# A two-part transformer on one core: recurrent block reordered, attention matmuls issued for two heads at a time

## The reference

```
for l in range(DEPTH):                                   # first block, DEPTH = 2
    h = rmsnorm(x, g_pre_mix[l])
    ...splits of h @ w_in[l]: attention (8 heads of 64), pooling, gating unit, convolution, gate logits
    merged = sum of 4 branches, each times sigmoid(gate)
    x = x + rmsnorm(merged @ w_out[l], g_post_mix[l])
    h = rmsnorm(x, g_pre_ffn[l])
    f = (silu(h @ w_ffn_gate[l]) * (h @ w_ffn_up[l])) @ w_ffn_down[l]
    x = x + rmsnorm(f, g_post_ffn[l])

# second block: recurrent block, MLP, attention of 16 heads of 64 over shared keys and values, MLP
u = rmsnorm(x) @ w_in; gate, rec = halves of u
rec = causal convolution of 4 taps + bias
r, i = sigmoid(rec @ w_gate + b)                         # 8 blocks of 128 channels
a = exp(-8 r softplus(-lam)); b = sqrt(1 - a*a) * (i * rec)
h = scan over time of h = a*h + b;  out = (gelu(gate) * h) @ w_out
```

## Time and profile before

| | us |
|---|---|
| median of 3 runs | 2925.27 (2917.92 to 2926.51) |
| the profiled execution's own time | 2922.88 |
| its span | 2921.2 |
| TensorE busy | 2798.7, mean granted clock 0.978 |
| GpSimd busy | 1336.7 |
| VectorE busy | 1254.6 |
| ScalarE busy | 1057.2 |

### The profile page before, as it was taken

One profiled execution on the slowest core, in us unless ns is written; L12 is line 12 of the kernel. 1 busy time (PEld: TensorE's weight loads), 2 busy tenths in 40 slices (PEclk: granted clock), 3 DMA queues, 4 the chain that ended last, 5 costly groups with the idle time before them and its releaser, 6 DMA issues.

```text
span 2921.2 us, 34310 instructions
## 1 busy us (share of the span) xinstructions
PE 2798.7 (96%) x12222; PEld 2233.8 (76%) x12222; DVE 1254.6 (43%) x1679; ACT 1057.2 (36%) x1555; POOL 1336.7 (46%) x1032
## 2 busy tenths in 40 slices
PE   8899998999998999997999988799999999999999
PEld 6677776888876777775888866588888885688887
DVE  5555455212246554555221267753224227552222
ACT  4344433222243344433222345433224346532222
POOL 5345542444443444453444444444444436544443
PEclk9999999999999999998999999899999997999999
DMA  4233222233332333321333322233333220133333
GB/s 136 79 94 99 89 88 71 87 95 100 94 95 80 94 94 94 94 88 60 98 95 100 96 84 80 65 94 96 98 93 129 80 83 4 37 94 95 100 93 101
DMA packets 72697, 259.13 MB, mean 89 GB/s; under 512 B 8192, under 2 KB 9088, under 8 KB 72448
## 3 DMA queue, kind: packets, MB, share of 16 engines
q1 hardware_dynamic: 71280, 254.17, 28.7%
q10 hardware_dynamic: 1296, 3.28, 0.3%
HBM read 255.31 MB, written 2.10 MB: 88 GB/s over the span
## 4 chain that ended last, share of the span: by engine, by line
issue 40%; PE 32%; POOL 24%; DVE 2%; ACT 1%; POOLq 0%; DVEq 0%
POOL w_lo L316 12%; POOL w_lo L318 12%; PE ps L764 9%; PE ps L766 9%; PE ps L765 9%; PE ps L864 2%; PE ps L852 1%; DVE XS L1648 1%; DVE fb L1647 1%; PE ps L845 1%; PE ps L1140 1%; PE ps L1142 0%; PE ps L1141 0%; ACT w_hi L345 0%; PE ps L1086 0%
## 5 line engine op out<-in xcount | busy, mean ns | idle before, releaser
L316 POOL TENSOR_TENSOR w_lo<-w_raw,w_hi 128x512 fp32r<-128x512 f32 x476 | 636.0, 1336 | 1526.0 <-ACT w_hi L345 1525.2
L764 PE MATMUL ps<-H_hi,w_hi 128*128 128x512 f32 x2240 | 905.0, 404 | 35.7 <-POOL w_lo L318 21.2
L765 PE MATMUL ps<-H_lo,w_hi 128*128 128x512 f32 x2240 | 877.0, 392 | 0.0
L766 PE MATMUL ps<-H_hi,w_lo 128*128 128x512 f32 x2240 | 876.6, 391 | 0.0
L345 ACT ACTIVATE w_hi<-w_raw 128x1024 fp32r<-128x1024 f32 x476 | 499.9, 1054 | 536.6 <-DMA w_raw<-w_all 536.2
L318 POOL TENSOR_TENSOR w_lo<-w_raw,w_hi 128x512 fp32r<-128x512 f32 x476 | 650.8, 1367 | 0.0
L764 PEld LDWEIGHTS ps<-H_hi,w_hi 128*128 128x128 f32 x2240 | 423.5, 189 | 150.6 <-POOL w_lo L318 25.7
L765 PEld LDWEIGHTS ps<-H_lo,w_hi 128*128 128x128 f32 x2240 | 423.9, 189 | 97.0 <-issue 12.2
L766 PEld LDWEIGHTS ps<-H_hi,w_lo 128*128 128x128 f32 x2240 | 423.3, 189 | 89.8
L764 PE MATMUL ps<-Y_hi,w_hi 128*128 128x512 f32 x1168 | 458.7, 393 | 31.6 <-POOL w_lo L318 27.2
L766 PE MATMUL ps<-Y_hi,w_lo 128*128 128x512 f32 x1168 | 456.1, 390 | 0.0
(11 more groups left out here) (232 smaller groups left out, 2588.9 us busy)
## 6 DMA issues: line engine op xcount, KB each, us to landing
w_raw<-w_all SPq DMA_DIRECT2D x476, 512.0 KB, 3.6
X<-xT SPq DMA_DIRECT2D x8, 256.0 KB, 6.7
rel_bias<-bias ACTq DMA_DIRECT2D x1, 2048.0 KB, 9.0
outT<-X SPq DMA_DIRECT2D x8, 256.0 KB, 3.2
sguw<-sgu_wT ACTq DMA_DIRECT2D x2, 256.0 KB, 4.6
sgub<-sgu_b ACTq DMA_DIRECT2D x2, 128.0 KB, 4.8
sgug<-sgu_g ACTq DMA_DIRECT2D x2, 128.0 KB, 5.5
CS<-cossin SPq DMA_DIRECT2D x1, 256.0 KB, 8.8
```

What stands on the lines that cost most here:

```text
L316: nc.gpsimd.tensor_tensor(w_lo[:, s, 0:UNIT // 2], w_raw[:, s, 0:UNIT // 2], f(w_hi[:, s, 0:UNIT // 2]), ALU.subtract).then_inc(w_lo_half, 1)
L764: MM(out, wh, xh, start=start, stop=False)
L765: MM(out, wh, xl, start=False, stop=False)
L766: return MM(out, wl, xh, start=False, stop=stop)
```

## The change

1. `values` of the first attention runs once for two heads: the matmuls of the even head (output rows 0 to 63) and the odd head (rows 64 to 127) alternate. The odd head's transposed probabilities go into `probs`. ScalarE and VectorE split the two heads' result together, 8 times instead of 16.
2. The second attention works in 16 units of two heads by two query tiles, (3, 0) or (2, 1), instead of 16 heads by four tiles. Scores alternate between array rows 0 to 63 and 64 to 127 and go to four PSUM banks, values alternate between output rows. The elementwise work is done for two heads in one instruction.
3. Feed-forward: the memset is gone, the first pass copies; the loop on VectorE is written out; ScalarE takes two more `tick`s ahead of the first silu.
4. `together` runs five tiles across the three units, and the last three tiles unit by unit.
5. Recurrent block: the first tap and the square are ScalarE's, the two gate units come after the 7th input unit and after the second gelu unit, square roots come in two groups of four, and the order on all three engines is new. The softplus of `lam` moves into layer 0's feed-forward.

```
             def together(u0, n, xh, xl, ready, squares, wide=5):
...
+                for k in range(wide):
+                    tile(k)
                     for u in range(u0, u0 + n):
+                        product(u, k)
+                for u in range(u0, u0 + n):
+                    for k in range(wide, DT):
+                        if u == u0:
+                            tile(k)
+                        m = product(u, k)
+                    m.then_inc(w_used, 1)
...
-            def values(out, Vt, h, prT):
+            def values(h):
                 o = 0
                 for i in range(4):
                     n = S - i * P
-                    m = MM(out[:, i * P:S], Vt[:, i, h * 64:(h + 1) * 64], prT[:, o:o + n], start=i == 0, stop=i == 3)
+                    for e in range(2):
+                        m = MM(ps[64 * e:64 * e + 64, 3, i * P:S], V1[:, i, (h + e) * 64:(h + e + 1) * 64], turned1(e)[:, o:o + n], start=i == 0, stop=i == 3)
+                    o += n
+                m.then_inc(pv_done, 2)
+            def scores(u):
+                m, w = u // 2, widths(u)
...
+                for s, j in enumerate(tiles_of(u)):
+                    for e in range(2):
+                        r = slice(64 * e, 64 * e + 64)
+                        if u == 0 and s == 1 and e == 1:
+                            pe.wait_ge(hn_sq, 16)
+                        i = MM(ps[:, 2 * s + e, S - w[s]:S], Q1[r, m, j * P:(j + 1) * P], K1[r, m, 0:w[s]], start=True, stop=True)
+                i.then_inc(s_ready, 1)
+            def values_pair(u):
+                big, small = tiles_of(u)
+                o = 0
+                for i in range(big + 1):
+                    c0 = 0 if i <= small else P
+                    n = 2 * P - c0
+                    for e in range(2):
+                        h = 2 * (u // 2) + e
+                        m = MM(ps[64 * e:64 * e + 64, 7, c0:2 * P], V2[:, i, h * 64:(h + 1) * 64], probsT2[:, u % 2, 5 * P * e + o:5 * P * e + o + n],
+                               start=i == 0, stop=i == big)
...
# VectorE, second attention, moved and maxima
-                link(VE.tensor_copy(probs2[:, g % 4, 0:P * 2], score(3, 0, P * 2)))
-                link(VE.tensor_copy(probs2[:, g % 4, S:S + P], score(2, 0, P)))
-                link(VE.scalar_tensor_tensor(kept(g, 0), score(0, 0, P), 1.0, rel_bias[:, h, P:2 * P], ALU.mult, ALU.add))
...
+                link(VE.tensor_copy(kept_pair(h, 0)[:, :, 0:w[0] - 2 * P], ps[:, 0:2, S - w[0]:2 * P]))
+                link(VE.scalar_tensor_tensor(kept_pair(h, 0)[:, :, w[0] - 2 * P:w[0]], ps[:, 0:2, 2 * P:S], 1.0, rel_bias[:, hs, :], ALU.mult, ALU.add))
+                VE.scalar_tensor_tensor(kept_pair(h, 1), ps[:, 2:4, S - w[1]:S], 1.0, rel_bias[:, hs, 2 * P - w[1]:2 * P], ALU.mult, ALU.add).then_inc(s_free, 1)
...
-                for j in range(4):
-                    link(VE.tensor_reduce(st[:, g % 2, 8 + j:9 + j], kept(g, j), AX.X, ALU.max))
+                for s in range(2):
+                    link(VE.tensor_reduce(st[:, g % 2, 8 + 2 * s:10 + 2 * s], kept_pair(h, s), AX.X, ALU.max))
...
# ScalarE, feed-forward
+                tick(U["ffn"] + 2)
+                tick(U["ffn"] + 3)
...
-                ffn(8, 0, U["ffn"], 0, 2)
+                ffn(8, 0, U["ffn"], 0, 4)
...
# VectorE, feed-forward
-                        VE.tensor_tensor(Dn[:, m, :], Dn[:, m, :], ps[:, c % 4, :], ALU.add).then_inc(unit_out, 1)
+                        if i == 0:
+                            VE.tensor_copy(Dn[:, m, :], ps[:, c % 4, :]).then_inc(unit_out, 1)
+                        else:
+                            VE.tensor_tensor(Dn[:, m, :], Dn[:, m, :], ps[:, c % 4, :], ALU.add).then_inc(unit_out, 1)
...
-                link(VE.memset(Dn[:], 0.0))
-                looped(2, 8, lambda i, lk: ffn(8, U["ffn"], i, 0, lk))
...
# ScalarE, recurrent block
+            def tap(k):
+                act.wait_ge(unit_out, U_REC[k] + 1)
+                nc.scalar.activation(rec[:, k, :], recp[:, k, 3:515], ACT.Identity, bias=v("a_conv_b", k), scale=v("a_conv", 24 + k)).then_inc(rec_tap, 1)
...
# TensorE, recurrent block
+            for k in (3, 4, 5):
+                rec_unit(k)
+            gates(0)
+            rec_unit(6)
+            gates(1)
+            rec_unit(7)
+            gelu_unit(0)
+            gates(2)
+            gelu_unit(1)
+            gates(3)
+            for n in range(2, DT):
+                gelu_unit(n)
```

More of the change, by code:

```diff
@@ L635, in _ @@
-            tick(L)
+            for k in range(3):
+                tap(k)
+            tick(B2 + 3)
+            tick(B2 + 4)
+            rec_hi(0)
+            rec_hi(1)
+            tap(3)
+            tick(B2 + 5)
+            rec_hi(2)
+            tap(4)
+            tick(B2 + 6)
+            rec_hi(3)
+            rec_hi(4)
+            tap(5)
             gates(0)
-            rec_hi(7)
-            tick(L + 1)
-            tick(L + 2)
+            tick(B2 + 7)
+            rec_hi(5)
@@ L664, in _ @@
-            lru_hi(6)
-            lru_hi(7)
+            tick(B2 + 14)
+            square((4, 5, 6, 7))
+            tick(B2 + 15)
+            sqrt((4, 5, 6, 7))
+            tick(B2 + 16)
+            for n in range(5):
+                gelu(n)
+            tick(B2 + 17)
+            lru_hi(0)
+            gelu(5)
+            lru_hi(1)
+            lru_hi(2)
+            gelu(6)
+            tick(UAO)
+            lru_hi(3)
+            lru_hi(4)
+            gelu(7)
+            for k in (5, 6, 7):
+                lru_hi(k)
@@ L781, in unit, with together, product, tile @@
                 m.then_inc(w_used, 1)
-            def together(u0, n, xh, xl, ready, squares):
+            def together(u0, n, xh, xl, ready, squares, wide=5):
                 pe.wait_ge(w_lo_ready, u0 + n)
                 pe.wait_ge(unit_out, u0 + n - 4)
-                for k in range(DT):
+                def product(u, k):
+                    s = u % WSLOTS
+                    return three(ps[:, s, :], w_hi[:, s, k * P:(k + 1) * P], w_lo[:, s, k * P:(k + 1) * P], xh(k), xl(k), k == 0, k == DT - 1)
+                def tile(k):
                     if squares:
@@ L867, in attention @@
[L867 removed]
+            def attention(g0, units):
                 def valued(g):
[L869 removed]
+                    u = g - g0
                     pe.wait_ge(pt_a, g + 1)
[L871 to L879 removed]
+                    if u:
+                        pe.wait_ge(lo_ready, SPLIT["att2"] + u)
+                    values_pair(u)
+                for g in range(g0, g0 + units):
+                    u = g - g0
+                    if u + 3 < units:
+                        scores(u + 3)
@@ L1570, in gelu_out @@
                 dve.wait_ge(gelu_in, n + 1)
-                for i in range(2 if n in (1, 3) else 1):
+                dve.sem_inc(unit_out, 1)
+                if n == 1:
                     dve.sem_inc(unit_out, 1)
```

310 lines of the change are left out of this document (177 added, 133 removed).

## The result

The changed kernel takes 2845.05 us (median of 4 runs, 2844.52 to 2847.0) against 2922.39 before in the same comparison: ratio 0.9737, 95% interval 0.9719 to 0.9755. The forecast was 2837 with a range of 2816 to 2868. The profiled executions, on which the sum was made, are 2922.88 and 2844.99 us: 77.9 us less, where 86.7 were forecast.

The account below looks back on a forecast made before the run. TensorE, busy 2798.7 of 2921.2 us, was taken as the bound, with VectorE setting one stretch. Terms of -19.5, -23.2, -1, -23 and -20 summed to -86.7 on 2922.9, giving 2837 with a range of 2816 to 2868.

Parts of the forecast that it names:

- First attention: Values of two heads: matmuls of 8 pairs overlap fully, 17.1 us, and 8 fewer goings in and out, 2.4; -19.5.
- The row of two records 0.01 us apart: L980 before the change: two heads' records start 0.01 us apart, taken with L996 as showing full overlap.
- The loss that would leave 1.6 times for a pair: First attention: the skill's packing figure would give a pair about 1.6 times, making the term some 4 us smaller.
- Feed-forward: Both layers' starts: weight splits ahead of the silu end TensorE's wait and the clock's fall; -23.2, bounds -17 and -24.
- Recurrent block: Third output unit's w_lo comes 21.7 us earlier, 1.4 for the next wait; -23, bounds -31 and -12.
- VectorE decides: Recurrent block: VectorE's 127.5 us stretch loses taps, squares, a 6.2 us wait and more; its end moves 24 to 27.
- GpSimd's contention stays: Recurrent block: the same units are split beside VectorE's stretch, and L1556 keeps its mean of 1139.
- Second attention: VectorE sets periods of about 4.8 us: ten win 11, low-clock front -8, tail 1; -20, bounds +9 and -28.
- The rival of a low clock throughout: Second attention: TensorE stays at 1.2 GHz, 7.0 us a unit, 9 us over before; 2866 in all, chance 0.12.
- Pairs that don't overlap: Both attentions: first attention gives only -2.4, second 0; 2874 in all, chance 0.08.
- alternation that drains the array: Both attentions: each alternation between tiles costs 0.3 us without overlap; 2946, slower than before, chance 0.03.
- the rival of new handovers: New handovers eat the stalls' gain: feed-forward keeps 4 us each, recurrent block -12; 2855 to 2860, chance 0.17.

## Why the prediction was right, and where it was off

**First attention** (-19.5, measured -20.0). Right in mechanism and size. The row of two records 0.01 us apart was the one to trust. That a pair overlaps because it alternates holds for 12.4 of it. L996 was misread: its halves stand 8 records by 8, and what it showed was the overlap of four records at each change, not the full one. The loss that would leave 1.6 times for a pair did not come: two heads take 2.30 us, as one did. Two slots together are 63.6 us where they were 66.1, as this term says; the slots of 33.7 and 31.1 among the prediction's signs are 1.2 too long for it.

**Feed-forward** (-23.2, measured -21.0). TensorE's wait of 8.5 us is gone in both layers, with the fall of the clock. The three weight units stood at 494.4, 497.0 and 506.7, that is 501.0, 503.6 and 513.3 on the clock of before; the forecast was 500.5, 503.4 and 512.1. The last has a margin of 0.5 us and not 1.4, and it held. The memset's 3.47 us, which the prediction told as part of the path of before, are on it only with the late ticks.

**Recurrent block** (-23, measured -15.9). The chain was right: the same third output unit, its split behind gelu 6, a wait of 10.8 us (forecast: 10), the clock falling as before, and another 1.4 at the next wait. The begin came 2.8 us earlier (forecast 2.5 to 3), and new waits cancelled old ones: idle time fell from 18.7 to 12.2, forecast 6.8 less. The step that failed is "VectorE decides. ... the change takes 8 taps of 1052 ns (8.4), 8 squares of 965 (7.7)". With the softplus that term was 17.8 us, and it measured 8.6. Those means held 6.2 us that were not the instructions' own but came from running beside GpSimd's subtractions; the prediction saw contention and wrote "GpSimd's contention stays", and then let a share of it go with the instructions that bore it. It stays in full, and grew by 3.3 us with the same 34 halves in a shorter stretch. The result lies between the bounds of -31 and -12.

**Second attention** (-20, measured -18.7). The three parts: from the first scores to the first transposes 22.9 to 15.4 us, -7.6 (forecast -8); the fifteen periods 87.8 to 74.2, -13.6 (forecast -11, with a period of 4.8 that is 4.54); and the tail from the last transposes 5.1 to 7.2, +2.1 (forecast -1). VectorE is busy 17.07 of 18.17 us, over nine tenths. GpSimd, called close behind, has as much (17.08), and where it splits two weight units it takes over; the prediction named these splits and gave them no time. The clock fell four times in place of once: for 10.2 and 6.8 us (2357.5 to 2367.7, 2388.2 to 2395.0), near the end for 3.4 (2429.2 to 2432.6) and in the tail for 6.8 (2439.4 to 2446.2), 26.5 of them in the stage, in place of 30.7. The last fall is the tail's +2.1: each of its two groups of values takes 2.40 us instead of 1.30, and where the clock stayed up, in the changed kernel with one-input low parts, the same tail is 4.9 us. The rival of a low clock throughout didn't come. That the sum of this stage came out near -20 is in part luck: the periods gave 2.6 us more than forecast and the tail 3.1 less. The kernels that don't edit this stage would put it at -19 to -23, so that the forecast is inside what one profile can tell.

**The rivals.** Pairs that don't overlap, and alternation that drains the array, are out by the rows at 186.69. The recurrent block gave 7.1 us less than forecast, where the rival of new handovers had put down 11, but not by handovers: what was missing was contention. Two slips in the arithmetic change little: 2836.2 and 2.4 make 2838.6 and not 2837, and the kernel would be slower from 0.2 us an alternation and not from 0.25.

## What to carry to other kernels

Before you count an instruction that is to be moved away, split its mean by what ran beside it: the shortest of its line is what goes, the excess belongs to the neighbour and falls on what is left. Where several edits aim at one wait, cost them together and one at a time: here the memset was worth nothing or 7 us, depending on the ticks. And when a wait is taken away, read which second wait ends behind it, and what the moved work will run beside: here the second wait ended 2.9 us earlier than the first, and 2.0 us later than it would have without GpSimd's moved work.

## What the runs showed of the hardware

- Matmuls to the two halves of the array's columns overlap also when they are issued one head behind the other, from the moment when the earlier head has four records left (184.53 to 188.39 us above). In order, 8 records a head cost 1.55 us a pair in the first attention and 0.70 in the second, and 6 records 0.48. Scores, which use the two halves of the rows with 4 records a head, lost nothing.
- GpSimd's two-input subtraction lengthens VectorE's SBUF instructions from 0.69 to as much as 1.68 us, the same GpSimd time spent on one-input instructions to 0.98 in one kernel and 1.14 in the other. VectorE's instructions that read PSUM stayed at 0.69 (L1702, 692 ns, L1683, 691 ns, beside GpSimd's 55.65 us of work).
- TensorE's clock fell or didn't fall at the same place in the program in different kernels with the same code up to it (at 22 us), and that is worth 1.6 us there. Differences of that size between stages mean nothing in a single profile.
